# A new order of work in the tail of each attention head of a two-layer decoder step

## The chip, the cores and the metric

The kernel runs on one core of a Trainium2 chip. A core has a matrix engine (TensorE, in the profile PE, and PEld for its weight loads), a vector engine (VectorE, DVE), a scalar engine (ScalarE, ACT), a general one (GpSimd, POOL) and a queue engine (SyncE, SP). They run side by side and wait for each other through semaphores. The metric is the time of one execution on the device in microseconds (us); of the kernel before it is 2530.91 us, the median of three runs from 2530.05 to 2532.09.

## The reference

Two layers work on a prompt of 1024 tokens and on 8 single sample tokens, with width 1024. Each layer adds a mixer (pooling and short convolution in layer 0, a state-space block in layer 1) and then a cross-attention into 256 memory rows with 4 heads of 256. Only the attention is touched here:

```python
def mem_xattn(h, mk, mv, wq, wo):
    b, L, _ = h.shape
    q = (h @ wq).reshape(b, L, XA_HEADS, XA_HEAD_DIM).astype(jnp.float32)
    s = jnp.einsum('blhd,bmhd->bhlm', q, mk.astype(jnp.float32)) * (XA_HEAD_DIM ** -0.5)
    p = jax.nn.softmax(s, axis=-1)
    o = jnp.einsum('bhlm,bmhd->blhd', p, mv.astype(jnp.float32)).astype(h.dtype).reshape(b, L, D_MODEL)
    return o @ wo
...
        x = x + mem_xattn(rmsnorm(x, norm_xa[l]), mem_k[l], mem_v[l], w_xa_q[l], w_xa_o[l])
```

The prompt's tokens share one memory; each sample token has its own cached keys and values (8 x 256 rows).

## The kernel before

Everything is float32. Each matrix operand is split in two float32r parts, hi and lo, and a product is three matmuls (hi·hi, hi·lo, lo·hi; helper `three`). Activations lie transposed, 128 features on the partitions and 1032 tokens (1024 + 8) along the row, and a product over them is cut in NCH = 3 matmuls of 344 columns.

Weights come in units of 128 x 1024 values through two slots. SP loads a unit (`w_raw`), POOL splits it with two instructions (`w_hi`, then `w_lo`), PE takes it (`take`). The first matmul of a unit marks the other slot as used (`w_used`), and that lets POOL split the next unit. Results go to two accumulators in PSUM, `acc[0]` and `acc[1]`; `begin(a)` waits (`moved`) until DVE or ACT has taken the earlier result out. `M0` and `M1` are two more banks.

Each engine has its own program, and nothing reorders it: the order of the text is the order of work. A head of the attention (`attention(l, h)`, four per layer, `n` counts them) goes like this on PE. For each of 8 tiles of 128 tokens: `scores(i)` (6 matmuls into M0 or M1), later `turn(i)`, which transposes the tile's probabilities into `acc[1]`, and `fill(i)`, a step of other work. In heads 0 to 2 a step is one k-step (9 matmuls) of the query projection of the next head: steps 0 to 7 make its first half in `acc[0]`, steps 8 to 15 its second. In the last head (`last`) steps 0 to 7 are instead half k-tiles of the output projection of head 2, whose input `y_hi, y_lo` is complete by then. `mix(half, k)` multiplies probabilities with values for half the tokens (6 matmuls). The output projection of the head itself follows in `out_unit`: a unit of four output tiles, each of 18 matmuls, two units per head, the second one of head 2 being the steps of the last head.

Beside this ACT does the exponentials (`exp(i)`), scales them (`normalize`), and takes out hi parts (`turned_hi`, `mix_out`, `queries`); DVE does the row minimum (`mx`), reciprocals, all lo parts (`turned_lo`, `mix_out`, `queries`), adds output tiles to the residual `x` (`add_tile`), and multiplies the sample tokens' queries `q_bc` with the cached keys (L2067, 16 products of 128x256 a head, in rows i = 2 to 7: 2, 2, 3, 3, 3, 3). The sample tokens' scores are `ss`, their probabilities `sp`, their output `so`; PE transposes `ss` at L1076, `sp` at L1084 and `so` at L1102, and L1095 multiplies with the cached values. The queries of the sample tokens travel over DRAM (`q_rows`) to all partitions (`q_bc`), issued by ACT.

Lines of the profile: L1039 scores, L1048 turn, L1058 mix, L762 step of heads 0 to 2, L1025 step of the last head, L978 out_unit, L994 query_rows; L627 and L630 POOL's split; L2030 q_lo, L2042 y_lo, L2048 pt_lo, L2092 the scaling of `sp`, L1883 add_tile.

## Time and profile before

| | us |
|---|---|
| median of three runs | 2530.91 |
| the profiled execution | 2528.74 |
| its span | 2526.9 |
| PE busy | 2317.9 (92%) |
| PEld busy | 2227.1 (88%) |
| DVE busy | 1248.3 (49%) |
| ACT busy | 658.2 (26%) |
| POOL busy | 863.4 (34%) |
| share of PE in the chain of waits | 78% |
| mean of one POOL instruction `w_hi`, `w_lo` | 1.941, 2.649 |

Busy times of several engines overlap, so they don't add up. The chain of waits is followed back from the last instruction; an engine's share in it is the part of the span in which the end waited for that engine. The mean granted clock of PE over the span is 0.957 of 2.4 GHz; it is granted at two levels, 2.4 and 1.2 GHz. The two attention stages lie at about 950 to 1200 us and 2220 to 2465 us of the span.

### The profile page before, as it was taken

The page shows a single profiled execution, that of the slowest core. Times are in us where ns is not written, and L with a number is a line of the kernel's source. Part 1 is how long each engine was busy: PE and PEld are TensorE (multiplying, and loading weights), DVE is VectorE, ACT ScalarE, POOL GpSimd, SP SyncE. Part 2 cuts the span into 40 slices and gives each one's busy share as a digit, 9 for nine tenths or more (in the row PEclk, how much of TensorE's full clock was granted, in tenths as well). Part 3 has the DMA queues.
Part 4 walks back from the last instruction along what each step waited for, and adds up shares of the span by engine and source line. Part 5 has one row for each costly group of instructions (what it writes and reads, how often), then busy time and mean ns, then how long its engine had stood idle before and what let it go on. Part 6 is the DMA issues. An engine that isn't in the chain of part 4 may idle for free.

```text
span 2526.9 us, 35308 instructions
## 1 busy us (share of the span) xinstructions
PE 2317.9 (92%) x14815; PEld 2227.1 (88%) x14815; DVE 1248.3 (49%) x1925; ACT 658.2 (26%) x1155; POOL 863.4 (34%) x448
## 2 busy tenths in 40 slices
PE   8989999999999988998779999999989996889986
PEld 7889999999999978887779899889989986888876
DVE  4644553333323263444626754862774485534444
ACT  4511100000000033222342442343343242232223
POOL 0044443434344323222124524443443442242220
PEclk9999999999999989999889999999999997899997
DMA  8621111111111114323012322421332241143221
GB/s 241 209 91 47 42 46 42 42 50 43 48 50 42 42 55 143 114 93 105 26 53 78 108 70 58 122 74 45 89 100 67 59 121 34 28 159 117 101 92 67
DMA packets 256633, 202.99 MB, mean 80 GB/s; under 512 B 7453, under 2 KB 239597, under 8 KB 255439
## 3 DMA queue, kind: packets, MB, share of 16 engines
q1 hardware_dynamic: 206296, 128.81, 17.5%
q10 hardware_dynamic: 50207, 72.35, 8.7%
q8 instruction: 93, 1.52, 0.3%
q14 instruction: 37, 0.30, 0.0%
HBM read 180.68 MB, written 21.14 MB: 80 GB/s over the span
## 4 chain that ended last, share of the span: by engine, by line
PE 78%; DVE 10%; ACT 5%; issue 3%; DMA 2%; POOL 2%; ACTq 0%; DVEq 0%; SPq 0%; POOLq 0%
PE acc L762 43%; PE acc L787 13%; PE acc L978 6%; PE acc L1058 2%; PE M L1039 2%; PE acc L1192 1%; PE acc L879 1%; PE acc L811 1%; PE M L802 1%; DVE o_lo L2298 1%; PE acc L1025 1%; DMA w_raw<-in_w_xa_k 1%; DVE sq_sum L1893 1%; PE acc L932 1%; POOL w_hi L627 1%
## 5 line engine op out<-in xcount | busy, mean ns | idle before, releaser
L627 POOL TENSOR_TENSOR w_hi<-w_raw,zero 128x1024 fp32r<-128x1024 f32 x153 | 297.0, 1941 | 1412.0 <-PE acc L762 881.5
L762 PE MATMUL acc<-h_hi,w_hi 128*128 128x344 f32 x2520 | 573.6, 337 | 26.6 <-POOL w_lo L630 20.3
L762 PE MATMUL acc<-h_lo,w_hi 128*128 128x344 f32 x2520 | 545.2, 325 | 0.0
L762 PE MATMUL acc<-h_hi,w_lo 128*128 128x344 f32 x2520 | 542.8, 324 | 0.0
L762 PEld LDWEIGHTS acc<-h_hi,w_hi 128*128 128x128 f32 x2520 | 429.8, 193 | 49.3 <-issue 25.2
L762 PEld LDWEIGHTS acc<-h_lo,w_hi 128*128 128x128 f32 x2520 | 435.2, 193 | 0.0
L762 PEld LDWEIGHTS acc<-h_hi,w_lo 128*128 128x128 f32 x2520 | 431.0, 192 | 0.0
L630 POOL TENSOR_TENSOR w_lo<-w_raw,w_hi 128x1024 fp32r<-128x1024 f32 x153 | 405.3, 2649 | 12.0
L1883 DVE TENSOR_TENSOR x<-acc,x 128x1032 f32<-128x1032 f32 x160 | 196.9, 1232 | 330.8 <-PE acc L787 253.5
L2131 DVE SCALAR_TENSOR_TENSOR xb<-raw,prm,xb 128x1024 f32<-128x1024 f32 x48 | 99.3, 2068 | 104.1 <-ACT xb L1615 103.0
L1642 ACT ACTIVATE dec<-dec,acs_p 128x128 f32<-128x128 f32 x256 | 78.1, 388 | 54.8 <-DMA dec<-acs_rows 54.8
L787 PE MATMUL acc<-o_hi,w_hi 128*128 128x344 f32 x384 | 82.2, 322 | 10.2 <-DVE o_lo L2298 8.7
L787 PE MATMUL acc<-y_hi,w_hi 128*128 128x344 f32 x384 | 81.8, 321 | 5.0 <-DVE y_lo L2017 5.0
L1519 ACT ACTIVATE prob<-M,mx 128x256 f32<-128x256 f32 x64 | 30.4, 474 | 214.4 <-DVE mx L2058 163.5
L879 PE MATMUL acc<-m_hi,w_hi 128*128 128x256 f32 x256 | 75.7, 296 | 10.9 <-DVE w_lo L1826 9.5
L787 PE MATMUL acc<-y_hi,w_lo 128*128 128x344 f32 x384 | 82.1, 323 | 0.0
L787 PE MATMUL acc<-o_lo,w_hi 128*128 128x344 f32 x384 | 81.9, 322 | 0.0
L787 PE MATMUL acc<-y_lo,w_hi 128*128 128x344 f32 x384 | 81.9, 322 | 0.0
L787 PE MATMUL acc<-o_hi,w_lo 128*128 128x344 f32 x384 | 81.9, 322 | 0.0
L787 PEld LDWEIGHTS acc<-o_hi,w_hi 128*128 128x128 f32 x384 | 64.5, 189 | 11.7 <-issue 7.2
L1993 DVE TENSOR_TENSOR cv<-acc,c_sb 128x1032 f32<-128x1032 f32 x8 | 9.9, 1233 | 129.8 <-PE acc L762 129.8
L879 PE MATMUL acc<-m_lo,w_hi 128*128 128x256 f32 x256 | 72.7, 284 | 0.0
(307 smaller groups left out, 3755.7 us busy)
## 6 DMA issues: line engine op xcount, KB each, us to landing
w_raw<-in_w_in_even SPq DMA_DIRECT2D x48, 512.0 KB, 3.8
w_raw<-in_w_in_odd SPq DMA_DIRECT2D x41, 512.0 KB, 3.9
cache<-in_cache_mem_k ACTq DMA_DIRECT2D x16, 1024.0 KB, 6.6
cache<-in_cache_mem_v ACTq DMA_DIRECT2D x16, 1024.0 KB, 5.1
dec<-acs_rows ACTq DMA_DIRECT2D x32, 512.0 KB, 4.9
w_raw<-in_w_xa_k SPq DMA_DIRECT2D x16, 512.0 KB, 5.2
w_raw<-in_w_xa_v SPq DMA_DIRECT2D x16, 512.0 KB, 4.3
w_raw<-in_w_out_even SPq DMA_DIRECT2D x16, 512.0 KB, 3.7
```

What stands on the lines that cost most here:

```text
L627: pool.tensor_tensor(hi, raw_ap, zcol.to_broadcast([P, width]), ALU.add).then_inc(w_hi_done, 1)
L630: pool.tensor_tensor(lo, raw_ap, hi.bitcast(F32), ALU.subtract).then_inc(done, 1)
L762: ins = pe.matmul(acc[a][:, n * 512:n * 512 + CH], wt[:, s, w], mv[:, k, n * CH:(n + 1) * CH], start=(k == 0 and j == 0), stop=(k == KT - ...
L787: ins = pe.matmul(acc[a][:, n * 512:n * 512 + CH], wt[:, s, at:at + P], mv[:, k, n * CH:(n + 1) * CH], start=(k == 0 and q == 0), stop=(k ...
L879: ins = pe.matmul(acc[s][:, 1024:1024 + NM], wt[:, s, w], mv[:, k, :], start=(k == 0 and j == 0), stop=(k == KT - 1 and j == 2))
L978: ins = pe.matmul(acc[a][:, n * 512:n * 512 + CH], wt[:, s, w:w + P], mv[:, k, n * CH:(n + 1) * CH], start=(k == 0 and q == 0), stop=(k == ...
L1039: ins = pe.matmul(MS[i % 2][:, 0:NM], a[:, k, i * P:(i + 1) * P], b[:, 0, k * NM:(k + 1) * NM], start=(k == 0 and j == 0), stop=(k == 1 an ...
L1058: ins = pe.matmul(mixed, a[:, 1, at:at + P], b[:, m, :], start=(m == 0 and j == 0), stop=(m == 1 and j == 2))
L1519: act.activation(prob[:, i % 2, :], MS[i % 2][:, 0:NM], ACT.Exp, bias=mx[:, i:i + 1], scale=-1.0, accum_out=rsum[:, i:i + 1]).then_inc(exp ...
L1642: ins = act.activation(dec[m % 3][:, e, :], dec[m % 3][:, e, :], ACT.Relu, scale=-1.0, bias=acs_p[:, c, h:h + 1])
L1883: dve.tensor_tensor(t3(x[:, m, :]), a3(a), t3(x[:, m, :]), ALU.add).then_inc(moved[a], 1)
L2131: ins = dve.scalar_tensor_tensor(out=dst[:, 0:TP], in0=raw[:, k:k + TP], scalar=sw[:, k, src:src + 1], in1=dst[:, 0:TP], op0=ALU.mult, op1 ...
```

## The change

Four things change in the text; no instruction is added or left out, only their order and the tiles' places.

- PE, heads 1 to 3: `all_moved` no longer stands before the first scores; scores 0 and 1 come first, then steps 0 and 1, and the wait for `acc[1]` stands before the first turning.
- PE, heads 0 to 2: steps 8 and 9 go ahead of turning 6, step 10 ahead of turning 7, step 11 ahead of `mix(1, 0)`.
- ACT, heads 0 to 2: the first query tile is taken out before the last exponential.
- Head 2's first output unit makes 2 tiles in place of 4 and its slot is held; the last head has 12 steps for six tiles in place of 8 for four. Steps 8 to 11 stand around turnings 6 and 7 and the `sp` matmuls. DVE adds tiles 2 to 5 in rows 1, 3, 5, 7, tile 6 behind the scaling of `sp`, and tile 7 between the last two `mix_out`.

```diff
-            def out_unit(hi, lo, sets, late=None, after_first=None):
+            held = [0]
+
+            def out_unit(hi, lo, sets, late=None, after_first=None, tiles=4):
 
                 s, marks = take()
-                for j in range(4):
+                held[0] = s
+                for j in range(tiles):
...
                         project_part(0, unit[0], marks, (k,))
-                    elif i < 8:
-                        j, k = i // 2, i % 2
+                    elif i < 12:
+                        j, k = (2 + i // 2) % 4, i % 2
                         marks = []
                         if i == 0:
+                            unit[0] = held[0]
+                        elif i == 4:
                             unit[0], marks = take()
...
                 pe.wait_ge(kv_split, 2 * n + 2)
-                all_moved(0)
-                all_moved(1)
+                if not h:
+                    all_moved(0)
+                    all_moved(1)
                 for i in range(TT):
-                    scores(i)
+                    if i != 1 or h == 0:
+                        scores(i)
+                    if i == 0 and h:
+                        scores(1)
                     if i == 6:
                         mix(0, 0)
+                    if i == 2:
+                        all_moved(1)
                     if 2 <= i < 7:
                         turn(i - 2)
                     fill(i)
...
                 ins.then_inc(ss_turned, 1)
+                fill(8)
+                if not last:
+                    fill(9)
                 turn(TT - 2)
-                fill(8)
+                fill(10 if not last else 9)
                 turn(TT - 1)
-                fill(9)
+                if last:
+                    fill(10)
                 pe.wait_ge(sp_ready, n + 1)
...
                 ins.then_inc(sp_turned, 1)
-                fill(10)
+                fill(11)
                 mix(1, 0)
-                fill(11)
...
-                    out_unit(hi, lo, (1, 0), late, lambda: query_rows(n + 1))
+                    out_unit(hi, lo, (1, 0), late, lambda: query_rows(n + 1), 4 if h < HEADS - 2 else 2)
...
# ScalarE
                     for i in range(TT):
+                        if i == TT - 1:
+                            if not last:
+                                queries(0, 0)
+                            else:
+                                for _ in range(6):
+                                    t.next(0)
                         exp(i)
...
                         if i == TT - 1:
-                            if not last:
-                                queries(0, 0)
-                            else:
-                                for _ in range(4):
-                                    t.next(0)
                             mix_out(0, 1)
...
-                        for m in range(KT if h < HEADS - 2 else KT // 2):
+                        for m in range(KT if h < HEADS - 2 else 2):
                             t.next((m + 1) % 2)
...
# VectorE
                         if last and i % 2:
-                            add_tile(4 + i // 2, 0)
+                            add_tile(2 + i // 2, 0)
...
                     dve.tensor_scalar(sp[0:NB, :], sp[0:NB, :], s4[0:NB, 3:4], None, ALU.mult).then_inc(sp_ready, 1)
+                    if last:
+                        add_tile(6, 0)
                     dve.wait_ge(sp_turned, n + 1)
...
                     mix_out(1, 0)
+                    if last:
+                        add_tile(7, 0)
                     mix_out(1, 1)
...
-                        for m in range(KT if h < HEADS - 2 else KT // 2):
+                        for m in range(KT if h < HEADS - 2 else 2):
                             add_tile(m, (m + 1) % 2)
```


PE in the tail of head 0, from the transposes of `ss` (L1076, in the changed kernel L1087) to turning 6 and on; L762 is a step. Before:

```order
L1076 MATMUL M<-table,ss 8x128 [waits ss_ready]
L1076 MATMUL M<-table,ss 8x128
L1048 MATMUL acc<-table,prob 128x128 [waits pt_ready,prob_ready]
L1048 MATMUL acc<-table,prob 128x128
L762 MATMUL acc<-h_hi,w_hi 128x344 [waits moved0,w_split1]
L762 MATMUL acc<-h_hi,w_hi 128x344 x2
L762 MATMUL acc<-h_lo,w_hi 128x344 x3
L762 MATMUL acc<-h_hi,w_lo 128x344 x3
L1048 MATMUL acc<-table,prob 128x128 [waits pt_ready,prob_ready]
L1048 MATMUL acc<-table,prob 128x128
```

The changed kernel:

```order
L1087 MATMUL M<-table,ss 8x128 [waits ss_ready]
L1087 MATMUL M<-table,ss 8x128
L762 MATMUL acc<-h_hi,w_hi 128x344 [waits moved0,w_split1]
L762 MATMUL acc<-h_hi,w_hi 128x344 x2
L762 MATMUL acc<-h_lo,w_hi 128x344 x3
L762 MATMUL acc<-h_hi,w_lo 128x344 x3
L762 MATMUL acc<-h_hi,w_hi 128x344 x3
L762 MATMUL acc<-h_lo,w_hi 128x344 x3
L762 MATMUL acc<-h_hi,w_lo 128x344 x3
L1053 MATMUL acc<-table,prob 128x128 [waits pt_ready,prob_ready]
L1053 MATMUL acc<-table,prob 128x128
```

Turning 6 (L1048, now L1053) stands behind two steps instead of ahead of them; the wait for `acc[0]` and the weights (moved0, w_split1) now comes right after the `ss` transposes.

PE at the start of head 1, from the last matmuls of head 0's output projection (L978, now L981) on; L1039, now L1044, is the scores. Before:

```order
L978 MATMUL acc<-y_hi,w_lo 128x344 x3
L1039 MATMUL M<-kv_hi,q_hi 128x256 [waits moved1,moved0,kv_split]
L1039 MATMUL M<-kv_lo,q_hi 128x256
L1039 MATMUL M<-kv_hi,q_lo 128x256
L1039 MATMUL M<-kv_hi,q_hi 128x256
L1039 MATMUL M<-kv_lo,q_hi 128x256
L1039 MATMUL M<-kv_hi,q_lo 128x256
L762 MATMUL acc<-h_hi,w_hi 128x344 [waits moved0,w_split0]
L762 MATMUL acc<-h_hi,w_hi 128x344 x2
```

The changed kernel:

```order
L981 MATMUL acc<-y_hi,w_lo 128x344 x3
L1044 MATMUL M<-kv_hi,q_hi 128x256 [waits kv_split]
L1044 MATMUL M<-kv_lo,q_hi 128x256
L1044 MATMUL M<-kv_hi,q_lo 128x256
L1044 MATMUL M<-kv_hi,q_hi 128x256
L1044 MATMUL M<-kv_lo,q_hi 128x256
L1044 MATMUL M<-kv_hi,q_lo 128x256
L1044 MATMUL M<-kv_hi,q_hi 128x256 [waits qrow_ready]
```

The first scores no longer wait for the accumulators, and the second scores (L1044, waiting for qrow_ready) follow them directly; the step with its wait for moved0 comes behind both.

DVE in the last head of layer 0, around the scaling of `sp` (L2092, now L2107); `x<-acc,x` is an addition of an output tile. Before:

```order
L2048 TENSOR_TENSOR pt_lo<-acc,pt_hi 128x2x128 [waits pt_hi_ready]
L2090 RECIPROCAL s_104<-s_104 8x1 [waits s_exped]
L2092 TENSOR_SCALAR sp<-sp,s_104 8x256 [waits srinv_ready]
L2094 COPY spt<-M 128x2x8 [waits sp_turned]
L2042 TENSOR_TENSOR h_lo<-acc,h_hi 128x512 [waits y_hi_ready] x2
L2100 TENSOR_TENSOR h_lo<-M,h_hi 128x2x4 [waits sy_hi_ready]
L2100 TENSOR_TENSOR h_lo<-M,h_hi 128x2x4
```

The changed kernel:

```order
L2063 TENSOR_TENSOR pt_lo<-acc,pt_hi 128x2x128 [waits pt_hi_ready]
L2105 RECIPROCAL s_104<-s_104 8x1 [waits s_exped]
L2107 TENSOR_SCALAR sp<-sp,s_104 8x256 [waits srinv_ready]
L1898 TENSOR_TENSOR x<-acc,x 128x1032 [waits result]
L2111 COPY spt<-M 128x2x8 [waits sp_turned]
L2057 TENSOR_TENSOR h_lo<-acc,h_hi 128x512 [waits y_hi_ready]
L1898 TENSOR_TENSOR x<-acc,x 128x1032 [waits result]
L2057 TENSOR_TENSOR h_lo<-acc,h_hi 128x512 [waits y_hi_ready]
```

Two additions have moved in: one directly behind the scaling of `sp`, one between the two low parts of the mix. Step 10 on PE needs the accumulator that the first of them frees.

## Rows read from the trace of the kernel before

**Rows 1.** Timeline of PE, tail of head 0 in layer 0 (start us, us, instructions, [idle before <-releaser]).
```profile
976.22 0.39 PE L1058 MATMUL acc<-pt_hi,kv_hi 128*128 128x512 f32 x1
...
977.81 0.38 PE L1076 MATMUL M<-table,ss 128*8 128x128 f32 x2
...
982.30 0.66 PE L1048 MATMUL acc<-table,prob 128*128 128x128 f32 x2 [4.11 <-DVE pt_lo L2048]
...
985.34 0.43 PE L1048 MATMUL acc<-table,prob 128*128 128x128 f32 x2
...
987.94 0.61 PE L1084 MATMUL M<-table,sp 8*128 8x8 f32 x4 [0.76 <-DVE sp L2092]
...
988.48 0.74 PE L762 MATMUL acc<-h_hi,w_hi 128*128 128x344 f32 x3
...
989.99 0.40 PE L1058 MATMUL acc<-pt_hi,kv_hi 128*128 128x512 f32 x1
...
1002.35 0.32 PE L978 MATMUL acc<-y_hi,w_hi 128*128 128x344 f32 x1
```

**Rows 2.** Timeline of PE, tail of head 2 in layer 0.
```profile
1118.33 0.38 PE L1076 MATMUL M<-table,ss 128*8 128x128 f32 x2
...
1128.93 0.61 PE L1084 MATMUL M<-table,sp 8*128 8x8 f32 x4
```

**Rows 3.** Timeline of DVE, tail of head 0; the last row is its second query tile.
```profile
979.99 1.23 DVE L2030 SCALAR_TENSOR_TENSOR q_lo<-acc,q_hi 128x1032 fp32r<-128x1032 f32 x1 [3.49 <-ACT q_hi L1495]
...
981.74 0.75 DVE L2048 TENSOR_TENSOR pt_lo<-acc,pt_hi 128x256 fp32r<-128x256 f32 x2
...
986.74 1.15 DVE L2092 TENSOR_SCALAR sp<-sp,s 8x256 f32<-8x256 f32 x1
...
1003.68 1.23 DVE L2030 SCALAR_TENSOR_TENSOR q_lo<-acc,q_hi 128x1032 fp32r<-128x1032 f32 x1 [4.87 <-ACT q_hi L1495]
```

**Rows 4.** Timeline of PE, from head 0 to head 1 of layer 0.
```profile
1024.85 0.64 PE L978 MATMUL acc<-y_hi,w_lo 128*128 128x344 f32 x3
...
1026.86 0.36 PE L1039 MATMUL M<-kv_hi,q_hi 128*128 128x256 f32 x1 [1.37 <-issue]
```

**Rows 5.** Timeline of PE, from head 2 to the end of head 3, layer 0.
```profile
1143.34 0.32 PE L978 MATMUL acc<-y_hi,w_hi 128*128 128x344 f32 x1
...
1173.34 0.50 PE L1058 MATMUL acc<-pt_hi,kv_hi 128*128 128x512 f32 x1 [0.95 <-DVE pt_lo L2048]
...
1183.06 0.41 PE L1048 MATMUL acc<-table,prob 128*128 128x128 f32 x2 [2.47 <-DVE pt_lo L2048]
...
1183.92 0.69 PE L1048 MATMUL acc<-table,prob 128*128 128x128 f32 x2 [0.44 <-ACT prob L1524]
...
1186.71 1.02 PE L1084 MATMUL M<-table,sp 8*128 8x8 f32 x4 [2.10 <-DVE sp L2092]
...
1196.97 0.42 PE L978 MATMUL acc<-h_hi,w_hi 128*128 128x344 f32 x1 [0.97 <-DVE h_lo L2042]
```

**Rows 6.** Timelines of DVE and POOL, last head of layer 0.
```profile
1168.24 0.41 DVE L2067 CUSTOM_DVE_ANT_0 cache<-cache,q_bc 128x256 f32<-128x256 f32 x1
...
1186.31 0.34 DVE L2092 TENSOR_SCALAR sp<-sp,s 8x256 f32<-8x256 f32 x1
...
1159.68 2.39 POOL L630 TENSOR_TENSOR w_lo<-w_raw,w_hi 128x1024 fp32r<-128x1024 f32 x1
```

**Rows 7.** Timelines of DVE and POOL in the state-space layer.
```profile
1405.59 1.12 DVE L2211 CUSTOM_DVE_ANT_0 bx<-st,bcs 128x128 f32<-128x128 f32 x1 [1.29 <-POOL st L703]
...
1405.51 1.05 POOL L695 TENSOR_TENSOR st<-st,dab 128x512 f32<-128x512 f32 x1
```

**Rows 8.** Windows: stretch, length; PE, PEld, DVE, ACT, POOL busy; clock, DMA, GB/s.
```profile
956.00:958.00 2.00, 2.00 (x9) 2.00 (x9) 0.42 (x1) 1.36 (x3) 1.00 (x1) 0.50 0.89 344
```

**Rows 9.** Timeline of ACT's queue (q_bc, last head), and the window where its DMA ends.
```profile
1149.54 0.35 ACTq L1504 DMA_DIRECT2D q_bc<-q_rows  x1
...
1154.00:1155.00 1.00, 1.00 (x7) 0.80 (x6) 0.00 (x0) 0.00 (x0) 0.00 (x0) 1.00 0.22 90
```

## The prediction

> **What bounds the kernel now.** I read the profile page first. Its table shows TensorE with 92% of the span busy and its chain of waits gives PE 78%, so a change counts as far as it shortens PE's own sequence; what DVE or ACT do costs only where PE stands. Then I read PE's timeline through the two attention stages (950 to 1200 us and 2215 to 2465 us) for rows that carry an idle time in brackets, and laid ACT's, DVE's and POOL's timelines beside it. Each layer has four heads, and the idles repeat: 1.37 before the scores of heads 1 to 3 [rows 4], 4.11 before turning 6 and up to 0.76 before the sample products in heads 0 to 2 [rows 1], and in the last head 0.95, 2.47, 0.44 and 2.10 in the middle and 0.97 at its end [rows 5]. I measure all steps from start to start, since an idle in brackets counts only from the modelled end of a matmul. A "step" is one `fill`, nine matmuls of 344 columns: 1.51 us (988.48 to 989.99 [rows 1]).
>
> **Heads 0 to 2, tail.** Between the transposes of `ss` and the matmuls on `sp` stand 10.13 us (977.81 to 987.94), and from there to the output unit 14.41 us [rows 1]. Head 2 has 10.60 for the first part [rows 2]; head 1 has 9.75, and layer 1 repeats the three within 0.04, so the six sum to 24.5 + 24.2 + 25.0 per layer, 147.4 in all. Now the new order.
> Step 8 needs `acc[0]` back from the queries. Step 15 ends where the output unit starts, 1002.35, and the q_lo behind it ends at 1003.68 + 1.23 = 1004.91, 2.56 later [rows 1, 3]. Step 7 ends at 976.22 [rows 1], and ACT is idle then (in the old order it stands at the last exponential, for turning 5), so q_lo ends at 978.8, where it was 981.2 [rows 3]. PE goes on at 978.9, 1.1 after the start of the `ss` transposes. Steps 8 and 9 take 3.0: 981.9.
> Turning 6 waits for pt_lo of tile 4, which ended at 982.1 (the pair starts at 981.74 [rows 3]). ACT's y_hi stood behind q_hi, which released q_lo at 979.9 [rows 3]; without these two instructions in front it starts about 1.0 sooner, 978.9, and takes 0.6. So y_lo follows at 979.5 and the first pt_lo ends at 980.6. So turning 6 has no wait at 981.9, step 10 ends at 983.5, and turning 7 follows.
> From turning 7 to the `sp` matmuls were 2.60 us (985.34 to 987.94 [rows 1]). In it the scaling of `sp` takes 1.15 [rows 3], in the last head 0.34 [rows 6]; POOL was splitting weights beside the long one and idle beside the short one. That split starts with the first matmul of step 8, now 3.4 us earlier, takes 4.3 and ends at 983.7, before the scaling at 984.9. So 1.8: `sp` at 985.3, which is 7.5 after `ss`. Of this 0.9 and 1.8 are still waiting; PE's stretch between them is 4.6 us of work.
> Behind it one step fewer is left: 14.4 − 1.5 = 12.9. Each tail becomes 20.4, and six save 147.4 − 122.4 = 25.0. About 1.4 of each is half clock that goes: turning 6 and step 8 took 3.04 (982.30 to 985.34) for 1.65 of work [rows 1].
>
> **Starts of heads 1 to 3.** The last output group starts at 1024.85, and three matmuls later, 1025.3, PE stands still for the last addition of a tile; scores start at 1026.86 [rows 4]. Scores 0 and 1 read neither accumulator. They take 1.43 together and go into these 1.53; step 0 waits for the same addition, for 0.1. Gain 1.4 a head. For heads 1 and 2, four in all, 5.7. POOL's split now begins 0.7 later against the first cache products, which stood right behind it: the first is held 0.7, in a step in which DVE has that much free, so I count nothing.
>
> **Last head.** From output unit to output unit are 53.63 (1143.34 to 1196.97 [rows 5]). Two tiles (5.7) leave head 2's end and four steps come back: no change. What changes is waits, from start to start. The start: −1.4. Turning 6: 2.7 before (its 2.47 and 0.25 of drain), step 8 covers 1.5 of it: −1.5. Turning 7's 0.44 and drain, 0.7, go under step 9. Then a new wait: step 10 needs `acc[0]`, and DVE adds tile 6 only behind `sp`: from turning 7 1.1 for the transposed tile and its low part, 0.5 for reciprocal and scaling, 1.2 for the addition, with 0.2 between engines 3.0, where the `sp` matmuls waited 2.5 (2.10 and a slow drain [rows 5]): +0.5. Sum −3.1 at equal clock. The old tail also ran 9.5 us at half clock, 3.3 too many.
> But POOL's next split moves too. It starts with the first matmul of the second unit: before, step 0, 4.3 us that ended (1159.68 + 2.39 [rows 6]) just before the first product; now step 4, at 17.6 after the output unit of head 2, and DVE's product of row 4 is due at 17.7 (1168.24 less the 1150.5 by which this stretch moves [rows 6]). Elsewhere in the trace a product with both inputs in SBUF met a POOL instruction: POOL ran 1405.51 to 1406.56, the product took 1.12 us where such take 0.29, and its end lies 0.15 behind POOL's [rows 7]. So a POOL instruction holds a product to its end. Two POOL instructions, 1.9 and 2.3: the products of rows 4 and 5 come up to 4.2 later, at least 3.0 if DVE gets three through first. DVE works without a gap there, and PE's mix(0,0), which had waited 0.95 for DVE [rows 5], comes 3.6 later, after 4.6 us idle.
> The Trainium skill (SBUF — State Buffer, "Who interferes with whom") states the same as an exclusive lock held for the whole instruction between a DVE instruction with two SBUF inputs and a GpSimd one that reads SBUF; without it the sum would be 7 us lower for the two layers and the half clock below would go too. The row agrees with it.
> All six idles of 4.1 were followed by half clock in at least the next steps, so this costs 1.6 here, as in head 0 above; the 2.8 idle before step 10 another 1.6 (below). Last head: −3.1 − 3.3 + 3.6 + 1.6 + 1.6 = +0.4, twice +0.8.
>
> **Clock.** 2.47 and 0.44 close together [rows 5] brought 1.2 GHz in both layers, 1.90 before the first scores in layer 0 (0.50 granted [rows 8]) but not in layer 1, 1.37 never in six. The new idles: 0.7 and 1.5 in six tails, 1 us allowed for one of them; 2.8 in each last head, counted as a fall.
>
> **Queues.** No DMA is added. q_bc for the last head now has less time: issued 6.2 after the output unit (1149.54), in by about 11.2, when the DMA engines fall quiet [rows 9]; first product due at 12.1. Margin 0.9, cost nothing. The second cache_v load is released behind the last exponential as before and needed 6 us later.
>
> **Sum.** −25.0 − 5.7 + 0.8 + 1.0 = −28.9 on the profiled execution, 2528.7 (its span 2526.9): 2499.8. The median of the runs is 2.2 above that execution, so 2502.
>
> **Rivals.**
> 1. The last head keeps its gain: POOL's split meets no product (it would have to start 1.2 later), or delays them without PE noticing. Then −6.4 twice in place of +0.8: −42.5, 2488. For it: POOL's start and the product's are 0.1 apart, and no row shows this product beside a split. Against: the split is 4.3 long and six products stand in it. Chance 0.17; a lock that costs half lies between.
> 2. The clock stays low: the new waits of 0.9 and 1.8 per tail still bring 1.2 GHz. Bounds: nothing, or 1.4 to 2.2 for each of six (head 2's slow stretch lasted 6.5 us), and 3.3 in place of 1.6 at the last heads. Gain 29 − 11 − 5 = 13: 2516. For it: 1.90 fell once. Against: 1.37 never did. Chance 0.18.
> 3. Slower: q_bc of the last head comes late. Each us behind 12.1 delays the products, turnings and PE one for one. In head 0 it took 7.2 from issue beside other loads, here 5; 7.2 would cost 1.3. It decides once it lands over 14 us late in both layers: 2535. Only a queue behind other megabytes could do so, and none is issued in that time. Chance 0.03.
> 4. The order makes no difference, because PE's idle moves on: if DVE, not ACT, held turning 6, the steps moved ahead would only be missed later. Each tail then keeps its 24.5 and only the starts pay, with the last head's loss: −4, 2527. q_lo, y_lo and pt_lo stand back to back on DVE, but all start with ACT. Chance 0.04.
> Forecast: 0.58.
>
> **How the numbers follow.** 0.2% is 5 us, about what a measurement of this kernel can tell. Faster: forecast, rivals 1 and 2, 0.93; same: most of rival 4, 0.03; slower 0.04. The range: the terms' bounds give 2488 (no lock, no half clock) to 2519 (half clock everywhere, lock 4.2); leaving a tenth at each end, 2490 to 2513.
>
> **What would show it.** In a tail: step 8 about 1.1 behind the `ss` transposes, no idle before turning 6, about 1.5 before `sp`, clock 1.00, `sp` scaling 0.34. At heads 1 to 3: scores directly behind the output tiles. Last head: one long product beside POOL's w_hi and one beside w_lo, mix(0,0) after over 4 us idle, and 2.8 idle before step 10. Wrong if tails last over 22 us, or if the last head is under 50 (rival 1) or over 57.

## The result, and the profile after

| | before | after |
|---|---|---|
| median of the runs, us | 2531.3 (4 runs, 2530.05 to 2532.09) | 2495.71 (4 runs, 2493.93 to 2497.36) |
| profiled execution | 2528.74 | 2494.27 |
| its span | 2526.9 | 2492.5 |
| granted clock of PE, mean | 0.957 | 0.965 |

(The 2530.91 given further up is the median of the first three of the runs before.) The ratio is 0.9863, 95% interval 0.9851 to 0.9874: faster by 1.4%, clear of the noise. 2495.7 lies in the forecast's range (2490 to 2513), 6 below its 2502. The page's table of busy times (share, instructions) and the chain's shares by engine:

```profile
PE 2302.7 (92%) x14815; PEld 2215.2 (89%) x14815; DVE 1251.9 (50%) x1925; ACT 659.3 (26%) x1155; POOL 864.6 (35%) x448
...
PE 77%; DVE 11%; ACT 5%; DMA 3%; issue 2%; POOL 2%; ACTq 0%; DVEq 0%; SPq 0%; POOLq 0%
```

PE does the same 14815 instructions, is busy 15 us less (fewer of them at half clock) and idle for 19 us less. PE's timeline shows where. The tail of head 0, against [rows 1]; L1087 transposes `ss`, L762 is step 8, L1099 the matmuls on `sp`, L981 the output unit; idle and releaser in brackets:

```profile
976.72 0.38 PE L1087 MATMUL M<-table,ss 128*8 128x128 f32 x2
977.84 0.70 PE L762 MATMUL acc<-h_hi,w_hi 128*128 128x344 f32 x3 [0.73 <-DVE q_lo L2045]
...
980.73 0.38 PE L1053 MATMUL acc<-table,prob 128*128 128x128 f32 x2
...
982.36 0.38 PE L1053 MATMUL acc<-table,prob 128*128 128x128 f32 x2
984.12 0.61 PE L1099 MATMUL M<-table,sp 8*128 8x8 f32 x4 [1.37 <-DVE sp L2107]
...
997.09 0.32 PE L981 MATMUL acc<-y_hi,w_hi 128*128 128x344 f32 x1
```

The idle of 4.11 before turning 6 (the first pair of L1053) is gone, and turnings 6 and 7 wait for nothing. From the `ss` transposes to the output unit are 20.37 us where 24.54 were. The clock of the same stretch, in a window (stretch, length; PE, PEld, DVE, ACT, POOL busy; clock, DMA, GB/s):

```profile
977.00:997.00 20.00, 17.89 (x129) 15.80 (x129) 5.48 (x15) 5.68 (x16) 8.88 (x6) 1.00 0.58 183
```

No half clock is left in it. At the start of head 1 the scores now follow the output tiles without the idle of 1.37 of [rows 4]:

```profile
1019.58 0.64 PE L981 MATMUL acc<-y_hi,w_lo 128*128 128x344 f32 x3
1020.06 0.28 PE L1044 MATMUL M<-kv_hi,q_hi 128*128 128x256 f32 x1
```

The last head of layer 0 on the same timeline, and two rows of layer 1, against [rows 5]; L1063 is the mix, L1053 a turning, L1030 a step:

```profile
1127.02 0.32 PE L981 MATMUL acc<-y_hi,w_hi 128*128 128x344 f32 x1
...
1153.04 0.50 PE L1063 MATMUL acc<-pt_hi,kv_hi 128*128 128x512 f32 x1 [4.05 <-DVE pt_lo L2063]
...
1161.45 0.38 PE L1087 MATMUL M<-table,ss 128*8 128x128 f32 x2
...
1164.30 0.41 PE L1053 MATMUL acc<-table,prob 128*128 128x128 f32 x2 [1.05 <-DVE pt_lo L2063]
...
1169.09 0.73 PE L1030 MATMUL acc<-y_hi,w_hi 128*128 128x344 f32 x3 [2.74 <-DVE x L1898]
...
1179.18 0.42 PE L981 MATMUL acc<-h_hi,w_hi 128*128 128x344 f32 x1 [0.98 <-DVE h_lo L2057]
...
2401.70 0.80 PE L1063 MATMUL acc<-pt_hi,kv_hi 128*128 128x512 f32 x1 [4.05 <-DVE pt_lo L2063]
...
2418.53 0.74 PE L1030 MATMUL acc<-y_hi,w_hi 128*128 128x344 f32 x3 [2.73 <-DVE x L1898]
```

Here two waits are new or longer: mix(0,0), which waited 0.95 before, now waits 4.05, and step 10 waits 2.74 for the addition of tile 6. Turning 6 waits 1.05, where it had waited 2.47. The windows of layer 0 behind the first and behind the second:

```profile
1155.00:1158.00 3.00, 3.00 (x15) 3.00 (x14) 0.69 (x1) 1.45 (x4) 0.00 (x0) 0.58 0.43 123
...
1169.00:1173.00 4.00, 3.91 (x23) 3.64 (x24) 0.21 (x2) 0.00 (x0) 0.00 (x0) 1.00 0.00 0
```

The clock fell behind 4.05 and not behind 2.74. Why DVE is late for the mix is seen in its own timeline beside POOL's. L2082 is a sample product (CUSTOM_DVE_ANT_0) and the read-out behind each (DVE_READ_ACCUMULATOR2_ANT), L2073 the next row's minimum:

```profile
1144.78 0.41 DVE L2082 CUSTOM_DVE_ANT_0 cache<-cache,q_bc 128x256 f32<-128x256 f32 x1
1145.12 0.08 DVE L2082 DVE_READ_ACCUMULATOR2_ANT ss<- 128x1 f32 x1
1145.12 2.11 DVE L2082 CUSTOM_DVE_ANT_0 cache<-cache,q_bc 128x256 f32<-128x256 f32 x1
1147.15 0.08 DVE L2082 DVE_READ_ACCUMULATOR2_ANT ss<- 128x1 f32 x1
1147.15 2.59 DVE L2082 CUSTOM_DVE_ANT_0 cache<-cache,q_bc 128x256 f32<-128x256 f32 x1
1149.67 0.08 DVE L2082 DVE_READ_ACCUMULATOR2_ANT ss<- 128x1 f32 x1
...
1150.01 0.41 DVE L2073 TENSOR_REDUCE mx<-M 128x1 f32<-128x256 f32 x1
...
1150.74 0.08 DVE L2082 DVE_READ_ACCUMULATOR2_ANT ss<- 128x1 f32 x1
1151.09 0.07 DVE L2082 DVE_READ_ACCUMULATOR2_ANT ss<- 128x1 f32 x1
```

```profile
1144.82 2.12 POOL L627 TENSOR_TENSOR w_hi<-w_raw,zero 128x1024 fp32r<-128x1024 f32 x1 [12.96 <-PE acc L1030]
1147.02 2.44 POOL L630 TENSOR_TENSOR w_lo<-w_raw,w_hi 128x1024 fp32r<-128x1024 f32 x1
```

Undisturbed, a product takes 0.41 and read-outs follow each other by 0.35 (1150.74, 1151.09). Beside the split two products take 2.11 and 2.59, one beside `w_hi` and one beside `w_lo`, and each ends 0.3 behind the end of that POOL instruction (1146.94 and 1149.46). The read-outs stand 2.03 and 2.52 apart. The two engines took turns: product, `w_hi`, product, `w_lo`, product. That is 3.85 us lost on DVE (2.03 and 2.52 less twice 0.35), all in row 4. Layer 1 has the same two products, 2.11 and 2.59.

Start to start, in us, layer 0 / layer 1 (SS: the `ss` transposes, OUT: the output unit, S0: the next head's first scores). The two tiles that the last head took over are 2.85 each (18 matmuls of 0.158, 997.09 on):

| | before | after |
|---|---|---|
| SS to OUT, heads 0, 1, 2 | 24.54, 24.19, 25.01 / 24.54, 24.15, 24.97 | 20.37, 20.43, 20.42 / 20.46, 20.43, 20.43 |
| OUT to S0, heads 0 and 1 (each) | 24.51 | 22.97 |
| S0 to SS, heads 1 and 2 | 21.39, 21.38 | 21.57, 21.57 |
| OUT (head 2) to S0 | 13.12 | 5.89 |
| S0 to SS, last head | 23.76 | 28.54 / 29.32 |
| SS to OUT, last head | 16.75 / 16.73 | 17.73 |
| whole stage, SS of head 0 to OUT of head 3 | 219.16 / 219.10 | 202.46 / 203.37 |

The stages give 32.4 of the span's 34.4.

### The profile page after: what moved, and what is told of

It is laid out like the page before. It is cut to its first block, busy times and chain, and to the rows that moved or that the text cites. A ratio compares the mean times of both kernels' runs of the same rounds, so it can differ in the third digit from the quotient of the medians.

```text
span 2492.5 us, 35310 instructions
## 1 busy us (share of the span) xinstructions
PE 2302.7 (92%) x14815; PEld 2215.2 (89%) x14815; DVE 1251.9 (50%) x1925; ACT 659.3 (26%) x1155; POOL 864.6 (35%) x448
## 4 chain that ended last, share of the span: by engine, by line
PE 77%; DVE 11%; ACT 5%; DMA 3%; issue 2%; POOL 2%; ACTq 0%; DVEq 0%; SPq 0%; POOLq 0%
PE acc L762 43%; PE acc L787 13%; PE acc L981 5%; PE acc L1063 2%; PE acc L879 1%; PE M L1044 1%; PE acc L1206 1%; PE acc L811 1%; PE M L802 1%; PE acc L1030 1%; DVE o_lo L2317 1%; DMA w_raw<-in_w_xa_k 1%; DVE sq_sum L1908 1%; POOL w_hi L627 1%; PE acc L932 1%
## 5 line engine op out<-in xcount | busy, mean ns | idle before, releaser
L762 PE MATMUL acc<-h_hi,w_hi 128*128 128x344 f32 x2520 | 568.8, 334 | 30.9 <-POOL w_lo L630 20.4
L762 PE MATMUL acc<-h_lo,w_hi 128*128 128x344 f32 x2520 | 541.3, 324 | 0.0
L762 PE MATMUL acc<-h_hi,w_lo 128*128 128x344 f32 x2520 | 539.0, 323 | 0.0
L762 PEld LDWEIGHTS acc<-h_hi,w_hi 128*128 128x128 f32 x2520 | 425.5, 191 | 55.3 <-issue 31.6
L762 PEld LDWEIGHTS acc<-h_lo,w_hi 128*128 128x128 f32 x2520 | 431.6, 191 | 0.0
L762 PEld LDWEIGHTS acc<-h_hi,w_lo 128*128 128x128 f32 x2520 | 427.1, 191 | 0.0
L787 PEld LDWEIGHTS acc<-o_hi,w_hi 128*128 128x128 f32 x384 | 64.5, 189 | 11.7 <-issue 7.2
L879 PE MATMUL acc<-m_hi,w_lo 128*128 128x256 f32 x256 | 72.4, 283 | 0.0
```

What stands on the lines that cost most here:

```text
L762: ins = pe.matmul(acc[a][:, n * 512:n * 512 + CH], wt[:, s, w], mv[:, k, n * CH:(n + 1) * CH], start=(k == 0 and j == 0), stop=(k == KT - ...
L787: ins = pe.matmul(acc[a][:, n * 512:n * 512 + CH], wt[:, s, at:at + P], mv[:, k, n * CH:(n + 1) * CH], start=(k == 0 and q == 0), stop=(k ...
L879: ins = pe.matmul(acc[s][:, 1024:1024 + NM], wt[:, s, w], mv[:, k, :], start=(k == 0 and j == 0), stop=(k == KT - 1 and j == 2))
```

## The experiments

Ten runs of nine kernels were made. Repeats of one kernel lie up to 6 us from their median. The clock is one reason: outside the two attention stages, where no edit acts, the traces have between 165 and 192 us at half clock. So each is judged by the stretches of its trace first, in the table's terms, and by its time second.

**Queries alone.** The kernel before, ACT takes the first query tile out ahead of the last exponential, and in the last head its four steps for output tiles (`t.next`) that stood in the same place:

```diff
                     for i in range(TT):
+                        if i == TT - 1:
+                            if not last:
+                                queries(0, 0)
+                            else:
+                                for _ in range(4):
+                                    t.next(0)
                         exp(i)
...
                         if i == TT - 1:
-                            if not last:
-                                queries(0, 0)
-                            else:
-                                for _ in range(4):
-                                    t.next(0)
                             mix_out(0, 1)
```

> The kernel before with one part of the change: ScalarE takes the first query tile out before the last exponential; PE's order is the old one. My theory (turning 6 waited for a chain that stood behind the queries on ACT and DVE): the idle before turning 6 falls from 4.11 to about 2.5 us, each of the six tails from 24.5 to about 22.5 (1.6 less wait, and half clock in only some of them), total -9 to -14 us. Rival (the chain is held by something else, the queries only stood in its shadow): idle stays 4.1 and the time stays within 3 us.

2517.7 in one run, beside 2529.3 of before. The idle and the window behind it:

```profile
982.97 0.41 PE L1048 MATMUL acc<-table,prob 128*128 128x128 f32 x2 [2.47 <-DVE pt_lo L2049]
```

```profile
984.00:987.00 3.00, 3.00 (x15) 2.94 (x14) 1.80 (x5) 0.98 (x4) 2.92 (x2) 0.56 0.32 105
```

The idle went from 4.11 to 2.47, all six tails are 22.51 to 22.54, the stages 212.7: as expected. Behind 2.47 all six tails still had a stretch at half clock.

**PE's steps alone.** The kernel before, in heads 0 to 2 steps 8 and 9 ahead of turning 6, 10 ahead of 7, 11 ahead of mix(1,0); ACT as it was.

```diff
+                if not last:
+                    fill(8)
+                    fill(9)
                 turn(TT - 2)
-                fill(8)
+                fill(10 if not last else 8)
                 turn(TT - 1)
-                fill(9)
...
-                fill(10)
+                fill(11)
                 mix(1, 0)
-                fill(11)
```

> The kernel before with one other part: in heads 0 to 2 PE has steps 8 and 9 ahead of turning 6, 10 ahead of turning 7, 11 ahead of mix(1,0); ACT's order is the old one. My theory: step 8 needs the accumulator that the queries leave at 981.3, so PE idles about 3.1 us in front of it (in place of 4.11 before turning 6), turning 6 has no wait, sp follows turning 7 by 1.8: tails of 22.8 at full clock, 24.2 if the 3.1 idle brings half clock, total -2 to -10. So neither part alone brings what both do (25). Rival (the parts add up independently): step 8 starts at once and the tails save about 3 us each, -18.

2516.1 in one run. The time fell by 13.2, more than the 2 to 10 expected, but the stages are 216.42 and 216.34 and give only 5.5 of it: 4.2 in the six tails and 1.3 in the two last heads, whose steps the edit leaves as they were. The other 7 us lie outside the stages, where no edit acts; between the stages this trace has 102 us at half clock where that of before has 113. PE now stands for the accumulator that the queries hold:

```profile
978.52 0.71 PE L762 MATMUL acc<-h_hi,w_hi 128*128 128x344 f32 x3 [3.18 <-DVE q_lo L2031]
```

```profile
978.00:981.00 3.00, 2.48 (x11) 2.51 (x12) 1.70 (x5) 0.66 (x2) 1.89 (x1) 0.70 0.61 212
```

Four tails kept a slow stretch (24.36 to 24.40), two did not (22.87, 22.89), as the expectation had priced them. An edit that removes an idle of 4.11 by putting work ahead of it gave 0.2 to 1.3 a tail, because that work waited 3.18 for the thing that the wait had also covered. Queries alone give 12.3 in six tails, steps alone 4.2, the changed kernel 24.9, and the changed kernel with the old starts (below) 20.4 and 21.8. So the two orders together give some 4 to 5 us more than the sum of the parts.

**Starts alone.** The kernel before, scores 0 and 1 first in heads 1 to 3.

```diff
-                all_moved(0)
-                all_moved(1)
+                if not h:
+                    all_moved(0)
+                    all_moved(1)
                 for i in range(TT):
-                    scores(i)
+                    if i != 1 or h == 0:
+                        scores(i)
+                    if i == 0 and h:
+                        scores(1)
                     if i == 6:
                         mix(0, 0)
+                    if i == 2:
+                        all_moved(1)
```

> The kernel before with one part alone: in heads 1 to 3 scores 0 and 1 come first, the wait for acc[1] before the first turning. Theory: the idle of 1.37 at the start of heads 1 to 3 goes and the tails stay at 24.2 to 25.0, since their clock falls behind the idle of 4.11 whatever stood before: three starts of 1.35 a layer, 8 in all, stage 219.2 to about 215.1, ratio 0.996 to 0.998. Rival (the idles of a head add up to the clock's fall): one or more of the tails loses its stretch at half clock too, 1.5 each, stage 211 to 214. Rival 2 (the last head takes its start back in its own waits for DVE): 2.7 a layer.

Ratio 0.9946 (0.9927 to 0.9966), 2517.7 against 2529.3. The stages are 213.66 and 213.52, 5.5 less each, between theory and rival: the starts give 1.36 in heads 1 and 2 and 1.4 in head 3, head 2's tail 0.9 and the last head's 1.3 more, because slow stretches were shorter; head 1's tail, at 24.91 and 24.79, took 0.7 back. The theory, that the tails stay as they were, and the rival, that one loses its slow stretch, both missed in part: every tail kept one, but the lengths changed. In the last head's tail, before and here:

```profile
1184.00:1193.00 9.00, 6.90 (x36) 4.14 (x40) 2.43 (x7) 1.55 (x5) 0.00 (x0) 0.50 0.13 43
```

```profile
1183.00:1192.00 9.00, 6.64 (x46) 4.18 (x46) 2.44 (x7) 1.77 (x6) 0.00 (x0) 0.62 0.11 37
```

**Starts back.** The changed kernel with that part undone (the edit above, reversed).

> The changed kernel with one part undone: heads 1 to 3 begin again with the waits for both accumulators, then scores 0, step 0, scores 1, step 1. Theory (a start is worth what stands in brackets, 1.37, because the accumulators come free later than the queries are ready): output unit to first scores back from 22.97 to about 24.4 in heads 0 and 1, and from 5.89 to 7.4 in head 2, first scores to ss 0.1 to 0.2 shorter: 1.3 to 1.4 for each of three starts a layer, 8 in all, stage 202.5 to about 206.5; whole time 2500 to 2505. Rival 1: the waits of the starts are covered by something else in the new order, so the starts cost nothing or up to 0.5 each. Rival 2: the last head's start gives nothing, since its POOL split and waits behind it take it up: 2.7 a layer.

Ratio 0.9957 (0.9942 to 0.9973), 2516.2, where the changed kernel has 0.9863. The three idles are back:

```profile
1026.31 0.36 PE L1044 MATMUL M<-kv_hi,q_hi 128*128 128x256 f32 x1 [1.37 <-issue]
```

They cost 1.35 to 1.5 each, as expected. But the stages are 209.7 and 211.0 and the time 2516.2, where 206.5 and 2500 to 2505 were expected: three of the six tails were 21.9 instead of 20.4, and the last head of layer 1 56.4 instead of 52.9. A window in the tail of head 1, behind the same idles of 0.73 and 1.37 that had brought nothing in the changed kernel:

```profile
1056.00:1059.00 3.00, 3.00 (x12) 2.75 (x11) 0.00 (x0) 0.00 (x0) 0.00 (x0) 0.56 0.33 99
```

Was that chance? The same kernel once more:

> The changed kernel with the old starts, once more, for a second profile. The first had three idles of 1.37 a layer, as expected, but also TensorE at half clock for about 3 us in three of its six tails, 1.5 each, behind the same idles of 0.73 and 1.37 that had brought none in the changed kernel. Theory A (the idle at the start of a head makes the clock fall at the tail 20 to 30 us later): of the six tails at least two are again 21.9 instead of 20.4, time 2510 to 2520. Theory B (chance): none or one of the six, time 2500 to 2508.

2512.8; two tails of six at 21.9, both last heads at 56.4. Over both profiles 5 of the 8 tails of heads 1 and 2, whose start has the idle, had a slow stretch, and none of the 4 of head 0, whose start is the same in all kernels. With the starts in the new order and the same tail (the changed kernel, tiles stay, slot marked later and tile 6 early) it was none of 16 in heads 1 and 2, and 1 of 8 in head 0. So theory A holds as far as counts go: the old start costs its idle and makes it likelier that a later idle brings half clock. The edit changes two things at a start, though, the idle of 1.37 and the order of scores and steps behind it, and no run has one without the other; so that it is the idle is argued, not shown. Not shown either is by what the chip decides it.

**Tiles stay.** The changed kernel with four tiles again in head 2's first unit and eight steps in the last head (the lines of ACT and DVE that follow from it are left out here):

```diff
-                    elif i < 12:
-                        j, k = (2 + i // 2) % 4, i % 2
+                    elif i < 8:
+                        j, k = i // 2, i % 2
...
-                    out_unit(hi, lo, (1, 0), late, lambda: query_rows(n + 1), 4 if h < HEADS - 2 else 2)
+                    out_unit(hi, lo, (1, 0), late, lambda: query_rows(n + 1))
```

> The changed kernel with one part undone: head 2's first output unit makes 4 tiles again, the last head has 8 steps, tiles 4 to 7 in it. Theory A (the moved tiles' gain is eaten by the 4.05 us idle before mix(0,0), where POOL's split meets the products): the last heads take 52.2 in both layers (53.6 less 1.4 at the start, old waits 2.47, 0.44, 2.10 and half clock), total within 2 us of the changed kernel. Rival B (the moved tiles are what made the last heads faster): last heads of 53.6 and total 2 to 3 us more.

2494.2, ratio 0.9860 (0.9835 to 0.9885): the same as the changed kernel. Last heads 51.48 and 51.89, so in the changed kernel the moved tiles cost 0.7 and 1.0; in the whole time that can't be told.

**Slot marked later.** The changed kernel, but POOL's split of the next unit is released by step 8 and no longer by step 4:

```diff
                         elif i == 4:
-                            unit[0], marks = take()
+                            unit[0], later[0] = take()
+                        if i == 8:
+                            marks = later[0]
```

> The changed kernel, but the first matmul of step 8 of the last head, not of step 4, tells POOL that the held slot is free; so POOL splits that unit after the 16 products. Theory A (a POOL instruction holds a product until its end): no product over 0.43 us, mix(0,0) idle falls from 4.05 to about 1.0, the last heads from 52.2 and 52.9 to about 48.5, total -7 to -8 us. Rival B (DVE is late by its own order or by q_bc, not by POOL): the idle stays 4.05 and the time too. What may come up: POOL's split now ends about 1 us before the scaling of sp; if it reached it, sp would take up to 1.2.

2491.1, ratio 0.9848 (0.9828 to 0.9869). POOL's split now stands behind the products, and the mix waits as it did before the change:

```profile
1150.65 0.50 PE L1066 MATMUL acc<-pt_hi,kv_hi 128*128 128x512 f32 x1 [0.95 <-DVE pt_lo L2066]
...
1165.16 0.74 PE L1033 MATMUL acc<-y_hi,w_hi 128*128 128x344 f32 x3 [2.73 <-DVE x L1901]
```

```profile
1158.21 1.89 POOL L627 TENSOR_TENSOR w_hi<-w_raw,zero 128x1024 fp32r<-128x1024 f32 x1 [25.65 <-PE acc L1033]
```

No product of this head takes over 0.43 now, as expected. Nothing else was changed, so the split beside the products was the cause of the 4.05; S0 to SS fell from 28.54 and 29.32 to 23.9. But the last head is 50.56, not 48.5, and the stages give 4.0 where 7 to 8 were expected, for this time the clock fell behind the 2.73:

```profile
1168.00:1171.00 3.00, 3.00 (x12) 2.98 (x12) 0.17 (x1) 0.00 (x0) 0.00 (x0) 0.50 0.00 0
```

It took 3.0 back: SS to OUT was 20.77, where the changed kernel has 17.73.

**Tile 6 early.** The kernel with the slot marked later, and in it DVE adds tile 6 ahead of the last pt_lo (the edit against that kernel):

```diff
+                    if last:
+                        add_tile(6, 0)
                     turned_lo(TT - 1)
...
-                    if last:
-                        add_tile(6, 0)
                     dve.wait_ge(sp_turned, n + 1)
```

> The kernel of the run with the slot marked at step 8, and in it one edit: in the last head DVE adds output tile 6 between the row sum of the samples and the last pt_lo, no longer behind the scaling of sp. There step 10 on PE stood 2.73 us (layer 0) for the end of that addition, which began 0.3 behind the start of the scaling at 1163.62, and PE's clock fell to half in the row behind. Theory (the addition's place is the wait): tile 6 is complete at about 1162.3, so the addition runs 1162.3 to 1163.5, the wait shrinks from 2.73 to about 1.0, no half clock follows, and transposes of ss to output unit goes from 20.8 to 17.3 or less; the last head from 50.56 to 46.5 to 47.5. sp is ready 0.6 later, which step 10 covers. Rival 1 (the clock falls behind the wait for turning 6 instead, 1.04 us, or by itself): the wait shrinks but a stretch at half clock stays, last head 48.5 to 50.5. Rival 2 (the late pt_lo holds turning 7's mix): a new idle before mix(1,0) of 0.5 or more. In the whole time 6 us less over two layers than the kernel with the mark at step 8 alone would be the theory, below what this chip's repeats (about 4 us) tell.

2482.7, ratio 0.9820 (0.9805 to 0.9835). The wait fell to 1.10, and the stretch behind it kept its clock:

```profile
1165.59 0.74 PE L1033 MATMUL acc<-y_hi,w_hi 128*128 128x344 f32 x3 [1.10 <-DVE x L1901]
```

```profile
1165.00:1173.00 8.00, 7.41 (x62) 5.68 (x63) 2.96 (x7) 0.99 (x3) 0.00 (x0) 1.00 0.26 66
```

Last heads 45.88 and 45.89, 0.6 under the expected. Of the 4.7 saved 1.6 is the idle and 3.0 the clock. One tail, head 0 of layer 1, had a stretch at half clock here (21.9).

**Step 11 ahead.** The kernel with tile 6 early, and in it step 11 stands ahead of the `sp` matmuls in heads 0 to 2 (the edit against that kernel):

```diff
-                if last:
-                    fill(10)
+                fill(10 if last else 11)
                 pe.wait_ge(sp_ready, n + 1)
...
                 ins.then_inc(sp_turned, 1)
-                fill(11)
+                if last:
+                    fill(11)
                 mix(1, 0)
```

> The kernel with tile 6 added early and, in heads 0 to 2, step 11 ahead of the matmuls on sp instead of behind them. In the changed kernel PE stood 1.37 there for DVE's scaling of sp (984.12), and a step takes 1.5. Theory: the idle goes wholly, nothing else moves: mix(1,0) (1.45 us) still covers DVE's copy of spt. ss to sp stays 7.4 to 7.6, ss to output unit falls from 20.4 to 18.9 to 19.1 in the six tails, 8 to 9 us in all. Whole time about 2480, 0.3 to 0.4% below the kernel with tile 6 early. Rival 1: the copy of spt now comes late, since only mix(1,0) stands between: an idle of 0.3 to 1.3 before the matmuls on the cached values, tails 19.3 to 20.4. Rival 2: the steps run out of weights: POOL's split of the slot comes late and a step waits by w_split, tails as before. Rival 3: step 11 in this place waits for nothing but the saved idle comes back at the output unit, which waits for h and xy.

2474.6 (5 runs, 2473.9 to 2477.35), ratio 0.9795 (0.9782 to 0.9809): 8.1 below tile 6 early on the same chip, and below the kernel before and the changed one. In the profiles the stages differ by 10.0: 1.5 of it is the stretch at half clock in the other kernel's one tail, 8.5 is the edit's. The tail of head 0; the idle before L1101, the matmuls on `sp`, is gone, and those on the cached values (L1112) still don't wait:

```profile
978.54 0.38 PE L1090 MATMUL M<-table,ss 128*8 128x128 f32 x2
...
985.93 0.61 PE L1101 MATMUL M<-table,sp 8*128 8x8 f32 x4
...
988.05 1.93 PE L1112 MATMUL M<-cache,spt 128*32 128x256 f32 x32
...
997.54 0.32 PE L982 MATMUL acc<-y_hi,w_hi 128*128 128x344 f32 x1
```

All six tails are 19.0, the stages 191.9 and 192.1. None of the three rivals showed.

**Tiles stay, step 11 ahead.** The changed kernel with four tiles again in head 2's first unit, eight steps in the last head, and step 11 ahead of the `sp` matmuls in heads 0 to 2.

> The changed kernel with the moved tiles undone (four tiles of head 2's first unit in head 2, eight steps in the last head), and step 11 ahead of the matmuls on sp in heads 0 to 2. Expected: last heads as in the run without moved tiles (51.5 to 51.9), tails 18.9 to 19.1 in place of 20.4. If the twelve steps are worth having once their waits are mended, the kernel with tile 6 early and step 11 ahead is below this one by the difference of the last heads, 4 to 5 us a layer, 8 to 10 in all; if the mends are worth nothing the two are equal.

2486.3, ratio 0.9836 (0.9821 to 0.9851); tails 18.98 to 19.01, last heads 50.78 (0.7 under the expected; why is not shown) and 51.57. Against step 11 ahead with twelve steps it is 4.9 and 5.7 a layer more, 11.7 in the time (expected 8 to 10). Moving the tiles is worth 10 us once its two new waits are mended, and nothing in the changed kernel as it stands.

## Why the prediction was right, and where it was off

**Tails: right.** 24.5 to 20.4 was forecast, 20.37 to 20.46 came. Step 8 at 1.1 behind the transposes: 1.12. No idle before turning 6: none. `sp` at 7.5: 7.40. Six tails gave 24.9, forecast 25.0. The scaling of `sp` was to fall from 1.15 to 0.34: it takes 0.34 in all eight heads. The two single-part runs show that the sum was rightly made of both edits: the idle's releaser was pt_lo, but pt_lo's own delay came from the queries, and each edit alone leaves a wait of 2.47 or 3.18. One thing the sum left out: with the old starts the same tails gave only 20.4 and 21.8. The forecast counted the starts' own 1.4 a head and nothing for what they do to the tails.

**Starts of heads 1 and 2: right.** 1.54 less before and 0.18 more behind, net 1.36 each; forecast 1.4. The first product there was held, as forecast, and ends 0.28 behind the POOL instruction (1024.16 + 2.39):

```profile
1025.88 0.95 DVE L2082 CUSTOM_DVE_ANT_0 cache<-cache,q_bc 128x256 f32<-128x256 f32 x1
```

It cost PE nothing.

**Last head: right in its mechanism, one term mis-sized.** +0.4 was forecast, −1.5 and −0.7 came. By terms, layer 0:

| term | forecast | measured |
|---|---|---|
| start | −1.4 | −1.5 (13.12 less 5.7 less 5.89) |
| mix(0,0) later, by the split beside the products | +3.6 | +3.1 (4.05 less 0.95) |
| half clock behind it | +1.6 | +1.5 (layer 1: +2.3), the rest of 28.54 less 23.76 with 0.2 for the scores' order |
| tail (turnings, step 10, old and new half clock) | −1.5 −0.7 +0.5 −3.3 +1.6 = −3.4 | −4.7 (17.73 less 5.7 less 16.75) |

The step that failed is the last: "the 2.8 idle before step 10 another 1.6". The idle came, 2.74, but no half clock in either layer, and without this 1.6 the tail's forecast is −5.0. Nor was 1.6 the right size when it did come: behind the same 2.73 the slot-marked kernel and three of the four last heads of starts back lost 3.0. So that term was not a sum but a draw between 0 and 3.0, and the honest forecast of the last head is +0.4 within 1.5. With 3.0 in both layers the time would have been about 2502, the very forecast, and by luck. The other size was the lock: 3.85 us of DVE against the forecast's 4.2, and PE's wait 4.05 against 4.6. The text said one long product beside each POOL instruction, and so it was: 2.11 beside `w_hi` and 2.59 beside `w_lo`. One product got through first, and so DVE lost 3.85.

**Clock allowance: not needed.** 1 us was set aside for half clock in the tails behind 0.7 and 1.4; none came. Rival 2, which had those idles bring half clock throughout, did not happen here. The two profiles with the starts back show that it was no idle fear: there 5 of 12 tails had it. Its time doesn't follow from its own terms: a gain of 13 gives 2518, not 2516.

**The rest.** Of the 5.5 between forecast (−28.9) and span (−34.4), the last heads are 3.0, the allowance 1.0, and some 2.0 lie outside the attention's stages, where no edit acts: 1.1 less before the first and 1.2 less between the two, 0.3 more behind the second. Tails and starts gave 0.4 less than forecast.

**Rival 1** (the last head keeps its gain, 2488) did not come: the split did meet the products. Its price left out the stretch behind step 10, which doesn't hang on the split: where the split was out of the way (slot marked later), the last head gained 3.1 and not 6.4, with 3.0 lost behind step 10. Nor would a split that starts 1.2 later have met no product: in that kernel row 5's three products start 2.3 behind row 4's (1147.80 and 1145.49), and a split lasts 4.3.

**Rival 3** (q_bc late) showed a beginning. Its bound, 14 us late, doesn't follow from its own rate: 28 us of delay only takes the forecast gain back. The prediction gave q_bc a margin of 0.9 us and counted 5 us from issue to landing; it took 7.3 (issued 1132.93, used 1140.27), and DVE's first product of layer 0's last head waited:

```profile
1132.93 0.35 ACTq L1518 DMA_DIRECT2D q_bc<-q_rows  x1
...
1140.27 0.42 DVE L2082 CUSTOM_DVE_ANT_0 cache<-cache,q_bc 128x256 f32<-128x256 f32 x1 [1.10 <-DMA q_bc<-q_rows]
```

It cost PE nothing that shows: the same 1.10 stands in the slot-marked kernel, whose mix waits 0.95 as before the change. DVE makes it up in the free time of these rows. But the margin was wrong by 2.0, and the rival nearer than 0.03 says.

**Rival 4** (the idle moves on) is what happens when PE's steps are moved alone: 4.2 in six tails instead of 24.9.

## What to carry to other kernels

Before work is moved ahead of a wait, list everything that the moved work itself needs and which other engine's instruction stands in front of that; here the steps needed an accumulator behind a late query copy, and alone the order on ACT was worth more (12.3) than the order on PE (4.2). When a slot changes hands elsewhere, the splitting that this releases moves too: place the release where the vector engine is not in products with two SBUF inputs, nor in a scaling that PE waits for. And small idles on TensorE are perhaps not independent: with the old starts the stages took 14.8 and 16.3 us more, of which the starts themselves are 8; the rest is half clock behind other idles.

## What the runs showed of the hardware that was not expected

- A POOL split and DVE products on SBUF alternated where both stood in a row: one product got through between `w_hi` and `w_lo`. A product beside them took 2.11 or 2.59 against 0.41. The POOL instructions were longer too, 2.12 and 2.44 beside the products against 1.89 and 2.38 alone.
- It is not only products with two SBUF inputs. Before the change the scaling of `sp`, which reads one tile of SBUF, took 1.15 in head 0 [rows 3] and ended at 987.89, 0.15 behind POOL's `w_lo`, whose row follows; in the changed kernel the split is over by then (982.73), and it takes 0.34 (983.72). A pt_lo, which reads one tile of SBUF and one of PSUM, took its usual 0.42 beside the same `w_lo` (986.23).

```profile
985.36 2.38 POOL L630 TENSOR_TENSOR w_lo<-w_raw,w_hi 128x1024 fp32r<-128x1024 f32 x1
```

- Half clock is not a function of the last idle. Behind 2.73 it came in 5 of 8 last heads (the changed kernel, slot marked later, starts back twice). Behind 0.73 and 1.37 it came in 1 of 24 tails with the new starts, but in 5 of 8 with an idle of 1.37 some 22 us ahead. In the six tails of steps alone it came three times right behind 3.18 and once only behind the 1.37 that follows. Behind 2.47 in a tail it came in 6 of 6. When it came it cost 1.5 in a tail and 3.0 in the last head.
